# Decay projections from stacked rounded parts, head norms by logarithm and exponential, and a last feed-forward layer with tokens as rows

## The chip, the core and the metric

The kernel runs on one core of a Trainium2 chip and is one launch. The metric is device time in microseconds (us). The engines are TensorE (PE, its weight loads PEld), VectorE (DVE), ScalarE (ACT), GpSimd (POOL) and SyncE (SP), which here only issues transfers.

## The reference, cut to what matters

Two blocks of a language model run one after the other on x of 1024 tokens by 1024 features, all float32. Three places of them matter here.

```python
# block 1, gated linear attention, 4 heads: key width 128, value width 256
log_a_f = log_sigmoid(lr_f @ w_decay_up_fwd + b_decay_fwd) / 16    # lr_f: 1024 x 16
log_a_b = log_sigmoid(lr_b @ w_decay_up_bwd + b_decay_bwd) / 16    # rank 16 -> 512
o = o * rsqrt(mean(o * o, axis=-1) + EPS)                          # per head and token, 256 wide
o = o * gla_norm * silu(r)
# end of block 2
y = square(relu(m @ w_up)) @ w_down                                # 1024 -> 4096 -> 1024
x = x + rmsnorm_2(y, norm_post_mlp)                                # mean of squares over 1024 features
```

## The kernel before, in words

Activations lie with features on the 128 partitions and the 1024 tokens along the row. A float32 product is made of three products of rounded parts ("hi" and "lo", type fp32r): hi by hi, lo by hi, hi by lo. Small products are plain float32 matmuls. Each engine has its instructions in a written order; semaphores join them. SP issues nearly all transfers, and when it waits, all its later transfers wait too.

**Paired projections** (`in_pe`, `in_dve`, `in_act`, L1126, 49 to 262 us): the first projections go in pairs of column tiles by a scheme of seven products (numbers r = 0 to 6) instead of eight; DVE makes each product's weight remainder (`in_lo`, L1087) four products ahead. The first decay product (`decay`, L1311) of head 0 stands within the last pair.

**Gated heads** (`gla_pe`, `gla_act`, `gla_dve`, 262 to 608 us): per head, PE runs five other projections (`mid_unit`, L572) with the head's small products between them. Per head there are two `decay` products, each two float32 matmuls of 64 rows by 512 columns; the ACT chain Abs, Exp, Ln and a DVE scan follow. After `output`, ACT squares the two value halves, DVE adds them into `mn`, and within `mid_unit(h, 4)` PE sums them per token (`sum_tokens`, L608, at k = 3), DVE makes mean and reciprocal and lays them on a diagonal (L1713, L1716, L620), PE spreads that over the partitions (`spread_tokens`, L614, at k = 6), ACT takes the root (L1627), and DVE applies norm, gain and gate (L1729, L1733). Then the last unit is evacuated by DVE (`evacuate`, L680) and the next head begins.

**Second feed-forward** (`f2_*`, 2040 us to the end): 16 hidden pairs (P2 to P2O - 1), then 16 output pairs (P2O to P2_LAST), seven products of 128x512 each (L3972; twelve matmuls a product). POOL makes weight sums and, in the hidden pairs, the weights' lo parts (L3868); ACT the hi parts. In the hidden pairs DVE posts the results (L3988, L3995, L4004), applies relu and the token's scale (L4237), and makes four differences of hidden blocks (`mix2_dve`, L4107); SP stores seven hidden blocks a pair. The output pairs take w_down as the stationary side (with its sums) and the hidden blocks and their differences as the moving side ("operands", `operand_load`, `operand_hi`, `operand_lo` L4049), seven of them changed every four pairs.

**End**: the output has features on partitions. In the last pair PE turns it (`end_turn` L4415, `end_turn_block` L4471), sums squares over partitions (`end_sum` L4489), ACT evacuates, DVE scales and adds the residual by rows (`end_rows` L4514), and SP stores eight rows of 512 KB.

Of the kernel before, what the change touches and what calls it, by code (L numbers as in the profile page):

```python
# [18 lines left out]
ALU = mybir.AluOpType  # L19
# [22 lines left out]
            ("norm_post_mlp_2", 8), ("b_decay_fwd", 4), ("b_decay_bwd", 4), ("conv_w_2", 16),  # L42
# [91 lines left out]
OUT2 = ((0, 4), (1, 2), (5, 6), (3, 7))  # L134
# [90 lines left out]
class Step:  # L225
# [23 lines left out]
    def landed(self):  # L249
# [18 lines left out]
        " x_added out_t out_ev x3_turned x3_out lr_landed row_squared").split()  # L268
# [7 lines left out]
         "t_hi": ("osq_ready", 8), "t_lo": ("z_min", 8), "h_floor": ("o_norm", 16), "h_square": ("gates_sig", 16),  # L276
         "h_mixed": ("o_gate", 16), "op_hi": ("o_hi", 8), "op_lo": ("o_lo", 8), "y_gained": ("sc_ready", 8),
         "out_row": ("kdt_ready", 8), "x3_squared": ("g_step", 4), "x3_summed": ("conv_step", 16),
         "logs_summed": ("xt_tr", 8), "logs_exp": ("xt_ev", 8), "qw_exp": ("vec_t", 2),
         "conv_loaded": ("norm_row", 18),  # L280
         "qw_zero": ("consts_ready", 7), "qw_made": ("f_log", 3), "ones_set": ("yb_ready", 8),
         "kt_turned": ("yb_scaled", 8), "kw_made": ("o_sum", 8), "u_made": ("lat_sum", 4),
# [9 lines left out]
         "e_turned": ("rmask_ready", 2), "e_inverse": ("wup_zero", 1), "o_weighed": ("row_squared", 6),  # L292
         "e_stored": ("lr_landed", 18), "e_landed": ("pool_consts", 2),
         "x3_last_spilled": ("mv_loaded", 64)}
# [3 lines left out]
            ("gla_loaded", 64), ("wpool_loaded", 16))  # L298
# [9 lines left out]
def two_block_kernel(nc, A, out):  # L308
# [29 lines left out]
    hid_d = dram("hidden2", (CH2 * 7 * 4 * P, HALF))  # L338
# [5 lines left out]
    with ctx:  # L344
# [47 lines left out]
        esum = sb("exponential_sums", [P, 120])  # L392
# [12 lines left out]
        with ExitStack() as s:  # L405
# [11 lines left out]
            wup = sb("wup", [64, 2, HALF], F32, s)  # L417
# [47 lines left out]
        rstd2 = at("rstd2", [P, T], 0)  # L465
        sqa, sqb_, ssqA, ssqB = [at(n, [P, T], R0 + kb) for n, kb in
# [5 lines left out]
        sqe, ssqe = at("sq_end", [P, 2, T], R0), at("sq_sum_end", [P, T], R0 + 8)  # L472
        ytok = at("y_turned", [P, KT, C, P], R0 + 48)
        x3t = at("x_by_token", [P, C, T], R0 + 96)
        orow = at("out_rows", [P, 4, T], R0 + 80)
        mask_row = at("mask_row", [P, T], R0 + 128)
        ylast = at("y_last", [P, 2, HALF], R0 + 16)
# [133 lines left out]

        def spread_tokens(pe, pair, diagonal):
# [85 lines left out]
        N_CONST = 7  # L698

        def start_pool(pool):  # L700
# [10 lines left out]
                               pattern=[[1, P]], channel_multiplier=-1).then_inc(S["consts_ready"], 1)  # L711

# [312 lines left out]
        def in_sp(sp):  # L1025
# [3 lines left out]
            for p in range(N_INP):  # L1029
                if p + 2 < N_INP:  # L1030
                    in_pair_load(sp, p + 2)
# [58 lines left out]
        def in_pool(pool):  # L1090
# [3 lines left out]
            for p in range(N_INP):  # L1094
                for which in (1, 3, 2, 4):
                    in_sum(pool, p, which)
# [3570 lines left out]
```

## Time and profile before

| | us |
|---|---|
| median of 3 runs (range) | 2645.98 (2641.83 to 2646.13) |
| the profiled execution itself | 2648.13 |
| its span in the trace | 2646.4 |
| paired projections, about | 49 to 262 |
| gated heads | 262 to 608 |
| hidden pairs of the second feed-forward | 2040 to 2310 |
| output pairs and end | 2310 to 2646.4 |

The span is the trace's, from the first to the last instruction; the rest of the execution's 2648.13 lies around it. A busy PE counts overlapping matmuls: what one costs is read from the start of one row to the start of the next.

### The profile page before, as it was taken

How to read it: one execution, taken by the hardware profiler on the slowest of the kernel's cores; microseconds unless marked ns; L12 is line 12 of the kernel's file. 1: busy time of each engine (PE TensorE's matmuls, PEld its weight loads, DVE VectorE, ACT ScalarE, POOL GpSimd, SP SyncE). 2: the span in 40 equal slices, each digit the busy share in tenths (PEclk: the TensorE clock that was granted, in tenths of full speed). 3: DMA queues.
4: the chain of work that ended last, by engine and by line, in shares of the span. 5: the costliest groups of instructions: out<-in, count | busy, mean ns of one | idle time of the engine just before them, and what ended most of it. 6: DMA issues, size and time to landing. Idle time of an engine off the chain costs nothing.

```text
span 2646.4 us, 32521 instructions
## 1 busy us (share of the span) xinstructions
PE 2585.6 (98%) x12370; PEld 2089.4 (79%) x12370; DVE 1841.8 (70%) x2062; ACT 1032.6 (39%) x1435; POOL 1213.3 (46%) x761
## 2 busy tenths in 40 slices
PE   8999999999999999999999999999999999999998
PEld 6888788887787888887877888676886888877777
DVE  8666655547658666668879657666658666778787
ACT  6223344333124333334435111765455333434444
POOL 2222222233437888885333343241136888733331
PEclk9999999999999999999999999999999999999999
DMA  5333323245331433345642352402333555744443
GB/s 202 121 111 106 119 96 128 89 151 167 129 134 56 119 104 102 94 136 196 226 132 64 125 171 96 132 17 93 109 100 100 156 150 153 236 156 139 159 144 143
DMA packets 337168, 341.35 MB, mean 129 GB/s; under 512 B 20099, under 2 KB 255270, under 8 KB 337014
## 3 DMA queue, kind: packets, MB, share of 16 engines
q1 hardware_dynamic: 331798, 319.87, 38.4%
q10 hardware_dynamic: 5216, 19.40, 1.9%
q8 instruction: 100, 1.64, 0.3%
q14 instruction: 54, 0.44, 0.1%
HBM read 230.38 MB, written 107.80 MB: 128 GB/s over the span
## 4 chain that ended last, share of the span: by engine, by line
PE 54%; DVE 8%; issue 3%; DMA 2%; ACT 1%; POOL 1%; SPq 0%; DVEq 0%; ACTq 0%; POOLq 0%
PE ps L3972 37%; PE ps L572 9%; PE ps L2991 2%; DVE op_lo L4049 2%; PE ps L3035 1%; PE ps L3015 1%; DVE sw_lo L3868 1%; DMA op_raw<-hidden 1%; PE ps L3534 1%; PE ps L3919 1%; DMA x_block<-acc 1%; DVE acc L2443 0%; DVE acc L4302 0%; DVE acc L4295 0%; DMA w_raw<-in_w_uq 0%
## 5 line engine op out<-in xcount | busy, mean ns | idle before, releaser
L3972 PE MATMUL ps<-op_hi,sw_hi 128*128 128x512 f32 x1765 | 690.9, 391 | 17.0 <-DVE op_lo L4049 6.8
L3972 PE MATMUL ps<-op_hi,sw_lo 128*128 128x512 f32 x1765 | 687.6, 390 | 0.0
L3972 PE MATMUL ps<-op_lo,sw_hi 128*128 128x512 f32 x1765 | 687.5, 390 | 0.0
L3972 PEld LDWEIGHTS ps<-op_hi,sw_hi 128*128 128x128 f32 x1765 | 331.7, 188 | 98.1 <-issue 16.6
L3972 PEld LDWEIGHTS ps<-op_hi,sw_lo 128*128 128x128 f32 x1765 | 331.7, 188 | 69.1
L3972 PEld LDWEIGHTS ps<-op_lo,sw_hi 128*128 128x128 f32 x1765 | 331.8, 188 | 68.6 <-issue 0.5
L538 POOL TENSOR_TENSOR w_hi_t<-w_raw,ones 128x1024 fp32r<-128x1024 f32 (+1 forms) x58 | 107.3, 1854 | 508.6 <-DMA w_raw<-in_w_in 242.2
L3858 ACT ACTIVATE sw_hi<-sw_sumNone 128x512 fp32r<-128x512 f32 (+1 forms) x252 | 157.0, 624 | 331.9 <-PE ps L3972 237.4
L3868 POOL TENSOR_TENSOR sw_lo<-sw_sumNone,sw_hi 128x512 fp32r<-128x512 f32 x138 | 214.4, 1563 | 34.5 <-ACT sw_hi L3858 34.4
L3819 POOL TENSOR_TENSOR sw_sumNone<-sw_raw 128x512 f32<-128x512 f32 (+1 forms) x63 | 113.9, 1808 | 227.4 <-DVE sw_lo L3868 196.8
L3858 ACT ACTIVATE sw_hi<-sw_raw 128x512 fp32r<-128x512 f32 (+1 forms) x188 | 116.8, 622 | 196.3 <-PE ps L3972 194.7
L3868 POOL TENSOR_TENSOR sw_lo<-sw_raw,sw_hi 128x512 fp32r<-128x512 f32 x109 | 157.8, 1449 | 53.2 <-ACT sw_hi L3858 53.2
L542 POOL TENSOR_TENSOR w_lo_t<-w_raw,w_hi_t 128x1024 fp32r<-128x1024 f32 (+1 forms) x58 | 151.0, 2607 | 4.1
L3834 POOL TENSOR_TENSOR sw_sumNone<-sw_raw,sw_sumNone 128x512 f32<-128x512 f32 (+1 forms) x63 | 92.0, 1461 | 87.5 <-DVE sw_lo L3868 84.8
L4004 DVE TENSOR_TENSOR hidden_blocks<-ps,s_u 128x512 f32<-128x512 f32 x111 | 76.1, 686 | 77.1 <-PE ps L3972 76.7
L3826 POOL TENSOR_TENSOR sw_sumNone<-sw_sumNone,sw_raw 128x512 f32<-128x512 f32 (+1 forms) x63 | 100.7, 1598 | 62.8 <-DVE sw_lo L3868 60.0
L4049 DVE TENSOR_TENSOR op_lo<-op_raw,op_hi 128x2048 fp32r<-128x2048 f32 (+1 forms) x49 | 119.6, 2443 | 6.8 <-ACT op_hi L4042 6.8
L3988 DVE TENSOR_TENSOR s_u<-ps,s_p 128x512 f32<-128x512 f32 x65 | 44.8, 689 | 110.1 <-PE ps L3972 110.0
L572 PE MATMUL ps<-m2hi,w_hi_t 128*128 128x512 f32 x304 | 106.4, 406 | 4.6 <-DVE m2lo L1546 2.1
L680 DVE TENSOR_TENSOR stage<-ps,rstd 128x1024 f32<-128x1024 f32 x36 | 43.9, 1220 | 90.2 <-PE ps L572 85.1
L572 PE MATMUL ps<-h1hi,w_hi_t 128*128 128x512 f32 x320 | 103.2, 404 | 0.0
L572 PE MATMUL ps<-m2lo,w_hi_t 128*128 128x512 f32 x304 | 101.7, 390 | 0.0
(514 smaller groups left out, 5415.5 us busy)
## 6 DMA issues: line engine op xcount, KB each, us to landing
op_raw<-hidden SPq DMA_DIRECT2D x42, 1024.0 KB, 8.9
w_raw<-in_w_in SPq DMA_DIRECT2D x47, 512.0 KB, 4.7
sw_raw<-in_w_ffn_in SPq DMA_DIRECT2D x44, 512.0 KB, 5.2
hidden<-hidden_blocks SPq DMA_DIRECT2D x13, 1536.0 KB, 6.1
hidden<-hidden_blocks SPq DMA_DIRECT2D x14, 1280.0 KB, 5.0
sw_raw<-in_w_up SPq DMA_DIRECT2D x32, 512.0 KB, 8.5
sw_raw<-in_w_down SPq DMA_DIRECT2D x32, 512.0 KB, 5.3
acc<-proj SPq DMA_DIRECT2D x28, 512.0 KB, 4.5
```

Of the source, the lines that this page charges most:

```text
L538: ins = pool.tensor_tensor(whi[:, u.par, s], raw[:, u.par, s], ones[:, 0:1].to_broadcast([P, n]), ALU.mult)
L542: ins = pool.tensor_tensor(wlo[:, u.par, s], raw[:, u.par, s], whi[:, u.par, s].bitcast(F32), ALU.subtract)
L572: mm = pe.matmul(out[:, b * HALF:(b + 1) * HALF], w, x[:, k, b * HALF:(b + 1) * HALF], start=(begin and k == ks[0] and n == 0), stop=(end ...
L2991: mm = pe.matmul(PS[n % 2][:, b:b + w], qT[0:96, h, i * P:(i + 1) * P], kT[0:96, h, b:b + w], start=True, stop=True)
L3819: pool.tensor_tensor(s1, a21, a22, ALU.add).then_inc(S["sw_sum"], 1)
L3826: pool.tensor_tensor(s2, s1, a11, ALU.subtract).then_inc(S["sw_sum"], 1)
L3834: pool.tensor_tensor(s2, a12, s2, ALU.subtract).then_inc(S["sw_sum"], 1)
L3858: act.activation(wshi[ring(m)][:, 0:n], weight_block(p, r), ACT.Copy).then_inc(S["sw_hi"], 1)
L3868: eng.tensor_tensor(wslo[ring(m)][:, 0:n], weight_block(p, r), wshi[ring(m)][:, 0:n].bitcast(F32), ALU.subtract).then_inc(S["sw_lo"], 1)
L3972: mm = pe.matmul(out, w, x[:, k, :], start=(k == 0 and i == 0 and r < 4), stop=(k == n - 1 and i == 2), skip_group_check=r >= 4)
L4004: dve.tensor_tensor(out, bank(p, r), u[:, :], ALU.add).then_inc(S["s_post"], 1)
L4049: dve.tensor_tensor(lo_of(first, r)[:, :, :], fresh_of(first, r)[:, :, :], hi_of(first, r)[:, :, :].bitcast(F32), ALU.subtract).then_inc(S ...
```

## The change

The decay columns: the low-rank activations are rounded once into `lr_parts` (128 rows: rounded part twice for the two weight parts already stacked, then its remainder, then the rounded part again), the decay weights into `w_parts` of the same 128 rows, by four ACT and three DVE instructions within the paired projections; `decay` becomes two fp32r matmuls of 128 rows by 512 columns. POOL clears `wup` once more and SP issues four more weight loads before pair 6's. In `in_dve` two evacuations and a small product change places around `t_lo(3)`.

The head norm: PE multiplies the squares by a matrix of ones on the stationary side (`spread_sums`, two float32 matmuls of 512 columns, at k = 3), which sums and spreads at once; ACT takes Ln with the mean's scale and the epsilon as bias, then Exp with scale -0.5. `sum_tokens`, `spread_norm`, and DVE's three instructions go.

The last layer: the hidden tiles are stored once (no differences) and loaded as the stationary side; w_down is the moving side, three of its blocks directly, four as differences that DVE makes in the hidden pairs (`down_load`, `down_mix`, `down_store`, one buffer). The output has tokens on partitions. So the squares' sums come from ACT's accumulator, root and reciprocal are of one column, the gain is a row loaded once, and the rows are finished and stored tile by tile in the last pairs. All turns and sums at the end go. Besides, four loads of block 2's value tiles are issued earlier (`mlstm_sp`), one vector is no longer turned, and semaphore counts move; these are left out below.

```diff
-OUT2 = ((0, 4), (1, 2), (5, 6), (3, 7))
+OUT2 = ((0, 4), (1, 5), (2, 6), (3, 7))
...
+        def spread_sums(pe, pair, squares):
+            for b in range(2):
+                mm = pe.matmul(PS[pair][:, b * HALF:(b + 1) * HALF], ones[:, :],
+                               squares[:, b * HALF:(b + 1) * HALF], start=True, stop=True)
+            return mm
...
-                    pe.wait_ge(S["gla_loaded"], 64)
-                    pe.wait_ge(S["unit_out"][0], 1)
+                    pe.wait_ge(*count("lr_part", 7))
...
+                if r == 4 and p in (1, 2, 6):
+                    (lr_high, lr_rounded, None, None, None, wup_rounded)[p - 1](act)
...
-                mm = pe.matmul(decay_bank(h, d)[:, b * HALF:(b + 1) * HALF], wup[:, d, h * P:(h + 1) * P],
-                               lrT[:, b * HALF:(b + 1) * HALF], start=True, stop=True)
+                mm = pe.matmul(decay_bank(h, d)[:, b * HALF:(b + 1) * HALF], w_parts[:, d * HALF + h * P:d * HALF + (h + 1) * P],
+                               lr_parts[:, b * HALF:(b + 1) * HALF], start=True, stop=True)
...
+        def lr_high(act):
+            act.wait_ge(S["unit_out"][0], 1)
+            act.activation(w_parts[0:64, :], lrT, ACT.Copy).then_inc(S["lr_part"], 1)
...
+        def lr_low(dve):
+            dve.wait_ge(*count("lr_part", 1))
+            dve.tensor_tensor(lr_parts[64:96, :], lrT[0:32, :], w_parts[0:32, :].bitcast(F32), ALU.subtract)\
...
+        def lr_rounded(act):
+            act.wait_ge(*count("lr_part", 2))
+            act.activation(lr_parts[0:64, :], lrT, ACT.Copy).then_inc(S["lr_part"], 1)
+            act.wait_ge(S["gla_loaded"], 64)
+            act.wait_ge(*count("lr_part", 3))
+            act.activation(lr_parts[96:P, :], w_rows[96:P, :], ACT.Copy).then_inc(S["lr_part"], 1)
...
+            dve.wait_ge(*count("lr_part", 4))
+            dve.tensor_tensor(w_parts[96:P, :], w_rows[96:P, :], lr_parts[96:P, :].bitcast(F32), ALU.subtract)\
+               .then_inc(S["lr_part"], 1)
+            dve.wait_ge(*count("lr_part", 5))
+            dve.tensor_copy(lr_parts[96:P, :], lr_parts[0:32, :].bitcast(F32)).then_inc(S["lr_part"], 1)
...
+            act.activation(w_parts[0:96, :], w_rows[0:96, :], ACT.Copy).then_inc(S["lr_part"], 1)
...
-                sum_tokens(pe, 3, [mn]).then_inc(S["o_sum"], 1)
-            def spread_norm(h):
-                pe.wait_ge(S["o_norm"], 4 * h + 4)
-                spread_tokens(pe, 3, mn).then_inc(S["o_sum"], 1)
+                spread_sums(pe, 3, mn).then_inc(S["o_sum"], 1)
-                mid_unit(h, 4, lambda k: square_sum(h) if k == 3 else spread_norm(h) if k == 6 else None)
+                mid_unit(h, 4, lambda k: square_sum(h) if k == 3 else None)
...
-                act.wait_ge(S["o_sum"], 2 * h + 2)
-                act.activation(mn[:, :], PS[3][:, :], ACT.Sqrt).then_inc(S["o_rstd"], 1)
+                if h == 0:
+                    act.wait_ge(S["consts_ready"], N_CONST + 1)
+                act.wait_ge(S["o_sum"], h + 1)
+                act.activation(mn[:, :], PS[3][:, :], ACT.Ln, scale=1.0 / 256, bias=eps).then_inc(S["o_norm"], 1)
+                act.wait_ge(S["o_norm"], 2 * h + 2)
+                act.activation(mn[:, :], mn[:, :], ACT.Exp, scale=-0.5).then_inc(S["o_rstd"], 1)
-                dve.wait_ge(S["o_sum"], 2 * h + 1)
-                dve.tensor_scalar(tok(0), by_tile(PS[3][:, :])[:, :, 0:1], 1.0 / 256, EPS, ALU.mult, ALU.add)\
-                   .then_inc(S["o_norm"], 1)
-                dve.wait_ge(S["o_norm"], 4 * h + 2)
-                dve.reciprocal(tok(0), tok(0)).then_inc(S["o_norm"], 1)
-                dve.wait_ge(S["o_norm"], 4 * h + 3)
-                diagonal(dve, mn[:, :], 0).then_inc(S["o_norm"], 1)
...
-                    out.append((w_down, (n1 * P, n2 * P), 8 * c, 4))
+                    out.append((hid2, (n1 * P, n2 * P), 8 * c, 4))
...
+            elif r in DOWN_BLOCK:
+                i, half = DOWN_BLOCK[r]
+                src = w_down[:, 8 * c + 4 * i:8 * c + 4 * i + 4, half]
+            else:
+                row = (4 * c + DOWN_DIFF.index(r)) * 4 * P
+                src = down_d[row:row + 4 * P, :].rearrange("(k p) t -> p k t", p=P)
...
-                    sp.wait_ge(*count2("h_mixed", 4 * (q + 1)))
-                    hidden_store(sp, q, q // 4, q % 4)
+                if 0 <= q < P2O - P2:
+                    sp.wait_ge(*count2("h_square", 4 * (q + 1)))
+                    sp.dma_start(hid2_tiles[q // 4, q % 4], hb2[q % 2][:, :, :]).then_inc(S["hid_stored"][q % 2], 16)
+                    if q < N_DOWN - 2:
+                        down_load(sp, q)
...
+                if p == P2O:
+                    down_load(sp, N_DOWN - 2)
+                if 0 <= q < N_DOWN - 2:
+                    down_store(sp, q)
+                if p == P2O + 1:
+                    down_store(sp, N_DOWN - 2)
+                    down_load(sp, N_DOWN - 1)
+                if p == P2O + 2:
+                    down_store(sp, N_DOWN - 1)
+                if p >= N_PAIR - 4:
+                    end_rows_sp(sp, p - N_PAIR + 4)
...
+        def down_load(sp, q):
+            if q:
+                sp.wait_ge(S["down_stored"], 32 * q)
+            for i in range(2):
+                sp.dma_start(wdown[i][:, :], down_tiles[q // 4, q % 4][:, i, :]).then_inc(S["down_landed"], 16)
...
+        def down_store(sp, q):
+            c, k = q // 4, q % 4
+            sp.wait_ge(*count("down_mixed", 4 * (q + 1)))
+            dst = down_d[16 * c * P:16 * (c + 1) * P, :].rearrange("(r k p) t -> p r k t", r=4, k=4)[:, :, k, :]
+            for i in range(2):
+                sp.dma_start(dst[:, 2 * i:2 * i + 2, :], wdown[i][:, :].rearrange("p (r t) -> p r t", r=2))\
+                  .then_inc(S["down_stored"], 16)
...
+        def down_mix(dve, q, steps):
+            blocks = {r: wdown[i // 2][:, HT[i % 2]] for i, r in enumerate(DOWN_DIFF)}
+            if steps[0] == 0:
+                dve.wait_ge(S["down_landed"], 32 * (q + 1))
+            for i in steps:
+                o, y = ((3, 2), (1, 3), (2, 1), (5, 1))[i]
+                if i in (1, 2, 3):
+                    dve.wait_ge(*count("down_mixed", 4 * q + min(i, 2)))
+                dve.tensor_tensor(blocks[o], blocks[o], blocks[y], ALU.subtract).then_inc(S["down_mixed"], 1)
...
-                if m in (N_SEQ - 6, N_SEQ - 5, N_SEQ - 3):
-                    n = 2 * (N_SEQ - 6, N_SEQ - 5, N_SEQ - 3).index(m)
-                    end_turn(pe, n)
-                    end_turn(pe, n + 1)
-                if m == N_SEQ - 2:
-                    end_turn_block(pe, 0)
-                    end_turn_block(pe, 1)
-                    end_sum(pe, 0)
-                    end_turn_block(pe, 2)
...
+            t = p - 1 - (N_PAIR - 4)
+            if t == 2:
+                for e in (4, 5):
+                    end_gain(dve, e)
+                for e in (4, 5):
+                    end_inverse(dve, e)
+                end_row(dve, 4)
...
-                end_adds(dve, p - 1)
+            if p in (P2O + 1, P2O + 2):
+                down_mix(dve, N_DOWN - 2 + p - P2O - 1, (0, 1, 2, 3))
+            if 0 <= t < 2:
+                end_gain(dve, 2 * t)
+            if p == P2_LAST:
+                end_block_gain(dve, 0)
...
-                end_gain(dve, 2)
-                end_scale(dve, 0)
-                end_rows(dve, 0, 2)
+                end_block_gain(dve, 2)
+                end_inverse(dve, 6)
+                end_row(dve, 6)
...
+                act.activation(sqe[:, :], acc[:, END_TILES[e], :], ACT.Square, accum_out=square_of(e)).then_inc(S["sq_done"], 1)
...
+            act.activation(deviation(e), square_of(e), ACT.Sqrt, scale=1.0 / D, bias=bias_of(e)).then_inc(S["rstd_ready"], 1)
...
+            dve.tensor_tensor(y_row(e), y_row(e), gain_row[:, :], ALU.mult).then_inc(S["y_gained"], 1)
...
+            dve.scalar_tensor_tensor(out=y_row(e)[:, a], in0=y_row(e)[:, a], scalar=inverse_of(e), in1=x3_row(e)[:, a],
+                                     op0=ALU.mult, op1=ALU.add).then_inc(S["out_row"], 1)
```

## Rows read from the trace of the kernel before

**Rows 1.** The page's parts 1 and 4: busy shares; the chain that ended last.
```profile
PE 2585.6 (98%) x12370; PEld 2089.4 (79%) x12370; DVE 1841.8 (70%) x2062; ACT 1032.6 (39%) x1435; POOL 1213.3 (46%) x761
...
PE 54%; DVE 8%; issue 3%; DMA 2%; ACT 1%; POOL 1%; SPq 0%; DVEq 0%; ACTq 0%; POOLq 0%
```

**Rows 2.** Windows view: span, then busy PE, PEld, DVE, ACT, POOL, clock, DMA.
```profile
62.00:249.00 187.00, 187.00 (x826) 154.89 (x826) 114.81 (x162) 47.85 (x78) 48.61 (x38) 1.00 0.39 121
...
276.00:362.00 86.00, 84.91 (x443) 70.54 (x444) 47.86 (x50) 33.38 (x31) 18.94 (x9) 1.00 0.32 104
...
2040.00:2310.00 270.00, 270.00 (x1191) 223.38 (x1192) 186.90 (x192) 107.54 (x175) 228.13 (x153) 1.00 0.57 174
```

**Rows 3.** Timeline of PE, first head: start, length, line, tile, count.
```profile
318.24 1.98 PE L1311 MATMUL ps<-ssq,wup 64*128 64x512 f32 x4
320.15 0.73 PE L572 MATMUL ps<-h1hi,w_hi_t 128*128 128x512 f32 x2
...
339.65 1.95 PE L608 MATMUL ps<-ones,mn 128*128 128x128 f32 x16
341.35 0.71 PE L572 MATMUL ps<-h1hi,w_hi_t 128*128 128x512 f32 x2
341.89 0.62 PE L572 MATMUL ps<-h1lo,w_hi_t 128*128 128x512 f32 x2
342.35 0.61 PE L572 MATMUL ps<-h1hi,w_lo_t 128*128 128x512 f32 x2
```

**Rows 4.** Timelines of ACT and DVE around the first head's norm.
```profile
322.49 1.28 ACT L1566 ACT_TABLE_LOAD   x1
...
347.44 1.03 ACT L1627 ACTIVATE mn<-ps 128x1024 f32<-128x1024 f32 x1 [6.14 <-PE ps L614]
...
348.50 1.28 DVE L1729 SCALAR_TENSOR_TENSOR kd<-ps,cols,mn 128x1024 f32<-128x1024 f32 x1 [5.21 <-ACT mn L1627]
```

**Rows 5.** Timeline of PE: waits at two head boundaries (in brackets).
```profile
364.72 1.09 PE L1459 MATMUL ps<-ident,kd 128*128 128x128 f32 x8 [1.00 <-DVE kd L1674]
...
609.31 0.73 PE L572 MATMUL ps<-m2hi,w_hi_t 128*128 128x512 f32 x2 [1.32 <-DVE stage L680]
```

**Rows 6.** Timelines of DVE and PE where the paired projections begin.
```profile
58.26 2.47 DVE L997 TENSOR_TENSOR acc<-ps,rstd 128x512 f32<-128x512 f32 x4
...
61.50 0.47 PE L1126 MATMUL ps<-h1hi,w_hi_t 128*128 128x512 f32 x1 [1.26 <-issue]
```

**Rows 7.** DMA issues, 2040 to 2310 us: KB each, median us to landing; DVE's mixes by form.
```profile
sw_raw<-in_w_up SPq DMA_DIRECT2D x26, 512.0 KB, 8.8
...
hidden<-hidden_blocks SPq DMA_DIRECT2D x7, 1280.0 KB, 5.0
...
L4107 DVE TENSOR_TENSOR hidden_blocks<-hidden_blocks,hidden_blocks 128x512 f32<-128x512 f32 x14 | 22.3, 1591 | 0.5
```

**Rows 8.** The end: two pieces of the chain, then timelines of PE and DVE, then DMA.
```profile
2610.49 1.75 PE ps L4415 x16
2612.23 2.74 PE ps L3972 x12
...
2626.54 0.60 PE L4471 MATMUL ps<-ident,acc 128*128 128x128 f32 x4
...
2629.95 0.48 PE L3972 MATMUL ps<-op_hi,sw_hi 128*128 128x512 f32 x1
...
2632.56 0.39 PE L3972 MATMUL ps<-op_hi,sw_lo 128*128 128x512 f32 x1
...
2638.09 4.87 DVE L4514 SCALAR_TENSOR_TENSOR out_rows<-y_turned,bytok,x_by_token 128x1024 f32<-128x1024 f32 x4 [0.81 <-ACT y_turned L4478]
...
out<-out_rows SPq DMA_DIRECT2D x8, 512.0 KB, 2.7
```

More of the change, by code:

```diff
@@ L698, in two_block_kernel @@
         N_CONST = 7
+        eps = small[:, 56:57]
         def start_pool(pool):
@@ L4218, in f2_act @@
                         square_act(act, p, i - 3)
-                    if p == P2_LAST:
-                        if i in (3, 4):
-                            end_block_act(act, i - 3)
-                        if i in (1, 2, 4):
-                            for n in range(2):
-                                end_evict(act, 2 * (1, 2, 4).index(i) + n)
+                    if p == P2_LAST and i in (3, 4):
+                        end_block_square(act, i - 3)
                 if p < P2O:
                     square_act(act, p, 3)
-        def mix2_dve(dve, q, steps):
-            dve.wait_ge(*count2("h_square", 4 * q + 4))
-            mix(dve, q, BEFORE2["h_mixed"] + 4 * q, steps)
         def hidden_dve(dve, p):
@@ L4481, in end_sum @@
-        def end_sum(pe, h):
-            pe.wait_ge(S["sq_added"], POST + 8)
-            pe.wait_ge(*count("s_post", posted(P2_LAST, "11")))
-            for n, src in enumerate((ssqe[:, HT[h]], block_square(2 + h))):
-                if n:
-                    pe.wait_ge(S["sq_done"], POST + 9 + h)
-                for c in range(4):
-                    mm = pe.matmul(PS[2][:, (4 * h + c) * P:(4 * h + c + 1) * P], src[:, c * P:(c + 1) * P], ones[:, :],
-                                   start=(n == 0 and c == 0), stop=(n == 1), skip_group_check=True)
-            mm.then_inc(S["norm_sum"], 1)
@@ new lines, in end_rows_sp @@
+        def end_rows_sp(sp, t):
+            if t == 0:
+                sp.wait_ge(*count("s_product", done(N_PAIR - 5, 6)))
+                sp.dma_start(gain_row[:, :], A["norm_post_mlp_2"][0].rearrange("(o n) -> o n", o=1).to_broadcast([P, T]))\
+                  .then_inc(S["gain_landed"], 16)
+                for e in range(2):
+                    x3_load(sp, e)
+                return
+            if t == 3:
+                sp.wait_ge(*count("s_product", done(P2_LAST, 0)))
+                for e in (6, 7):
+                    x3_load(sp, e)
+            for e in (2 * t - 2, 2 * t - 1):
+                row_store(sp, e, e)
+                if t < 3:
+                    x3_load(sp, e + 2)
@@ L4539, in end_sp @@
+            end_inverse(dve, 7)
+            for h in range(2):
+                end_row(dve, 7, h)
         def end_sp(sp):
-            for c in range(C):
-                sp.wait_ge(*count("out_row", c + 1))
-                sp.dma_start(out[0, c * P:(c + 1) * P, :], orow[:, c % 4, :]).then_inc(S["out_stored"][c % 4], 16)
+            row_store(sp, 6, 6)
+            for h in range(2):
+                row_store(sp, 7 + h, 7, HT[h])
             for i in range(4):
-                sp.wait_ge(S["out_stored"][i], 16 + 16 * C // 4)
+                sp.wait_ge(S["out_stored"][i], 16 + 16 * ((9 + 3 - i) // 4))
```

356 lines of the change are left out of this document (175 added, 181 removed).

## The prediction

> **What bounds the kernel now.** I read the page's busy shares first: PE is busy 98% of the span, DVE 70%, POOL 46% [rows 1]. The chain that ends last runs on PE for 54% of the span, and none of its other engines has more than 8% [rows 1]. The view by windows shows where another engine could take over: in the paired projections PE is busy 187.0 of 187 us with DVE at 115 and ACT at 48, around the first gated head 84.9 of 86 with DVE at 47.9, and of the second feed-forward 270.0 of 270, with POOL at 228 and DVE at 187 [rows 2]. So a matmul that leaves PE is worth its whole slot, provided that what follows it on ACT and DVE does not become late, and anything that delays PE in the hidden pairs is a loss. Only the last 13.5 us, behind the last product (2632.56 + 0.39 = 2632.95), are not PE's: there DVE writes rows and the stores land [rows 8].
>
> **Decay columns.** One decay product takes PE from 318.24 to 320.15, 1.91 us [rows 3]. It becomes two fp32r matmuls of 512 columns, the same as a pair of L572 matmuls, whose starts lie 342.35 - 341.89 = 0.46 us apart [rows 3]. Saved: 1.45 us, eight times = 11.6 us. Bounds for the new product, which the trace does not have: 0.46 us, and 1.91 us if it were no faster than the float32 one; I take the near row, since form and columns are those of L572. The new preparation is four ACT and three DVE instructions of up to 1024 columns. An ACT pass of that width is 1.03 us, a DVE one 1.28 [rows 4]. They stand at five places in a stretch where ACT is busy 48 and DVE 115 of 187 us [rows 2], and a remainder is made some three products of 2.7 us ahead of its use; that lead hides them, and I cost them at nothing. Without that cover they would cost 4 x 1.03 + 3 x 1.28 = 8 us. SP's four extra issues come while it waits for the sixth pair's slot anyway. POOL's second clearing stands between two pairs' sums.
>
> **Start of the paired projections.** PE waits 1.26 us until 61.50 for DVE's next remainder, which comes behind four evacuation halves (58.26 + 2.47 = 60.73) [rows 6]. Two of the halves now stand before `t_lo(3)`, in an idle spot, two behind the remainder. Bounds 0 and 1.26; I take 1.2.
>
> **Head norm on PE.** The sum per token costs 341.35 - 339.65 = 1.70 us and lengthens the next pair to 0.54 (341.89 - 341.35) instead of 0.46: 1.78 [rows 3]. The new matmuls have the form of the old spread, two float32 ones of 512 columns against ones, only earlier and with the sides changed. So one of the two steps goes, and the other stays at its price. Saved 1.78 us, four times = 7.1; bounds 0 (if the new step cost both) and 1.91, the other float32 pair of that width [rows 3].
>
> **Head norm on ACT and DVE.** Before, the root starts at 347.44 and ends at 348.47, and DVE, after 5.21 us of waiting, applies the norm at 348.50 [rows 4]. Now the sums are ready at 341.4; Ln of about 1.05 ends at 342.6; a table load of 1.28 [rows 4] and Exp of about 1.05 follow: 345.0. So DVE is 3.5 us earlier against PE, where PE itself comes 1.8 us earlier. The table load between the two is what the trace shows between Exp and Ln in the decay chain (322.49) [rows 4]. The Trainium skill, "ScalarE: Activation LUTs", section "Table sets: the hidden batching unit", says that one set holds both ln and exp, one load for the two. By that rule the norm would be ready 1.28 us sooner still, and the sum would be the same, since PE does not wait for it. The existing Exp and Ln show a load between them, so I follow the row.
>
> **What is late next in the heads.** At a head's start PE waits 1.00 us for `kd`, behind the evacuation of the unit that PE has just finished [rows 5]. That moves with PE and stays. After the last head PE waits 1.32 us for an evacuation [rows 5], which also follows its own unit; there ACT must do five more passes, two loads, Ln and Exp, and ends about when the evacuation does. I cost that at 0, bounds 0 and 1.3. Heads and projections together: 11.6 + 7.1 + 1.2 = 19.9 us.
>
> **The last layer, product by product.** Numbers and shapes of products, weight sums and operands are unchanged, so are DVE's four differences a pair, and the stationary side is still 512 KB a tile. In the hidden pairs SP now stores 1 MB of hidden tiles and moves 1 MB of w_down in and out, where before it stored 1.8 MB: 1.2 MB more a pair of 19 us, at a DMA share of 0.57 [rows 2]. One buffer serves load, mix and store, so there is a loop. With 5.0 us for a store of 1.3 MB [rows 7] a store takes about 4.5 us and a load of 1 MB about as long. From the first mix, which is behind the fifth product, to the last, 6.7 us go by (four at 1.59 [rows 7] and small gaps). Sum 15.7, below the pair's 19.0 (7 products of 2.72). Upper bound: 7 for the store, 8.8 for the load (the weights' landing) [rows 7], 7.3 for the mixes at 1.59 each: 23. I take no loss. The differences for the last two tiles go behind products in the second and third output pair; the two-pair margin hides them. The value tiles' earlier loads of block 2 wait for nothing PE needs: 0.
>
> **The end.** In the last pair PE turns three times two tiles at 1.75 us each and then spends 2629.95 - 2626.54 = 3.4 us on the block turns and sums [rows 8]: 8.7 us that go. The pair's products take 7 x 2.72 (a product is 2.74 in the chain [rows 8]) = 19.0 us, so it starts at T0 = 2632.95 - 19.0 - 8.7 = 2605. DVE comes into it at about T0 + 3.3, behind the fourth row. Its new order before the last post: two gains of 1.22 (4.87 / 4, [rows 8]), four small steps of 0.2, three rows of 1.28, and fourteen half-width steps (remainders, posts, half gains) of 0.65 (2.47 / 4 = 0.62 for such a one, [rows 6]): 2.4 + 0.8 + 3.8 + 9.1 = 16.1. That is T0 + 19.4; with some 1 us of waits within I take T0 + 20.4, 1.4 us behind the last product. Then post 0.7, ACT's last half square about 0.8 with its readout, root 0.2, reciprocal 0.2, two half rows 1.4: T0 + 23.7. From the last row to the end went 2646.4 - (2638.09 + 4.87) = 3.4 us; a store lands in 2.7 [rows 8], and a half one in no more: 3.2. End at T0 + 26.9 = 2631.9: 14.5 us saved. Bounds: 16 if DVE is on time and the half store quicker, 8.7 - 1.5 = 7 if the new tail is as long as the old one and DVE delays PE in it.
>
> **Sum.** 19.9 + 14.5 = 34.4 us off the profiled execution's 2648.1 gives 2613.7; the median of the runs is 2.1 below that execution, so 2612 us (2645.98 - 34.4 = 2611.6).
>
> **Rivals.**
> - A, the loop of load, mix and store is longer than a pair. For it: a single buffer, and 8.8 us landings [rows 7]; against it: most bytes are in rows of 2 and 4 KB, and the weights' loads come after the new load. Each us above 19.0 costs 14 us over the hidden pairs, less some 6.5 us of DVE's lead (about 2.4 products of 2.72, an estimate). At 20.5 us a pair: 14.5 lost, 2626. From 19.0 + (34.4 + 6.5) / 14 = 21.9 us on, the kernel is slower than before; at the upper bound of 23 it loses 49.5 us: 2661. That is the case of the other sign.
> - B, the heads keep less of what PE gives up: the chain from decay to `ks`, or the weights' load and split behind the evacuations, becomes the bound at each head. For it: PE already waits at each head's start [rows 5]; against: those waits follow PE's own units. If half of the heads' 18.7 goes, 2621.
> - C, the new end is DVE's: gains and rows (8 passes more over three pairs) delay posts, and PE waits. 5 to 7 us of the 14.5 lost: 2618.
> - D, the stacked product is no faster (it does not do what it says): 11.6 lost, 2623.
> - E, two input passes of DVE collide less or more with POOL than now: a mix has 1.59 us against 0.62 for a half-width step elsewhere [rows 6, 7]. This is within +-3 of the forecast.
>
> **How the numbers follow.** Forecast with E: 0.68, own range 2607 to 2617. B 0.09, C 0.10, D 0.03, A mild (2615 to 2640) 0.06, A slow 0.04. The range reaches from 2606 to 2624, which leaves out the slow cases and the strong forms of B and D. About 0.2% can be told from no change (5 us). Faster: 0.95; within: 0.01; slower: 0.04.
>
> **What would show it.** Decay rows of PE with next starts 0.46 us on; no L608 in the heads; Ln and Exp of 1.05 us with a table load between them and DVE's norm 3.5 us closer to the sum; waits at `kd` as now; PE busy 270 of 270 in the hidden pairs with no wait on a posted block, and down loads that land before DVE's fifth post; from the last product to the end 7 to 8 us instead of 13.5. The prediction is wrong if PE shows waits in the hidden pairs, or if the last pair takes more than 20 us.

## The result, and the profile after

The changed kernel takes 2615.44 us (median of 4 runs, 2612.77 to 2617.83) where the kernel before takes 2646.0. The ratio is 0.9889, 95% interval 0.9874 to 0.9905. The forecast was 2612, its range 2606 to 2624. The profiled execution took 2615.75 us with a span of 2614.0, 32.4 less than before in both, where 34.4 was forecast.

The busy shares hardly move: PE stays at 98% and lost 34 us of busy time; DVE gained 16. Columns are those of [rows 1].

```profile
PE 2551.7 (98%) x12194; PEld 2066.4 (79%) x12194; DVE 1857.9 (71%) x2060; ACT 1026.0 (39%) x1442; POOL 1214.3 (46%) x763
```

The windows that answer to [rows 2]: the paired projections, the first head, the hidden pairs, and the start of the output pairs.

```profile
62.00:249.00 187.00, 186.78 (x825) 154.62 (x825) 120.98 (x165) 53.07 (x84) 50.67 (x39) 1.00 0.39 119
276.00:362.00 86.00, 83.94 (x446) 71.33 (x445) 48.56 (x47) 37.28 (x35) 26.21 (x12) 1.00 0.37 119
2020.00:2290.00 270.00, 269.64 (x1190) 223.28 (x1191) 196.44 (x187) 102.18 (x171) 226.85 (x152) 1.00 0.67 226
2290.00:2340.00 50.00, 43.74 (x169) 32.26 (x168) 36.18 (x39) 18.19 (x23) 12.20 (x8) 0.97 0.68 231
```

Within these 270 us the hidden pairs are as full of PE as before, with the DMA share at 0.67 instead of 0.57. The fourth row is new: of 50 us PE is idle 6.3, and the granted clock is 0.97 of full. That is where the change loses.

The same matmul, found in both traces, shows where the 32.4 us come from. A product starts with the first of its matmuls.

| PE reaches | before | after | gained so far |
|---|---|---|---|
| second product of the paired projections | 61.50 | 59.17 | 2.3 |
| end of the last head | 605.53 | 587.79 | 17.7 |
| first hidden pair | 2036.46 | 2013.48 | 23.0 |
| first output pair's operands | 2314.83 | 2293.25 | 21.6 |
| its first products over | 2331.22 | 2314.70 | 16.5 |
| the end of the last product | 2632.95 | 2606.79 | 26.2 |
| end of the span | 2646.4 | 2614.0 | 32.4 |

The third place lies at a wait that only the kernel before has there. The changed kernel has one of its own two products later. The first row is the kernel before, the second the changed one:

```profile
2036.46 0.50 PE L3972 MATMUL ps<-op_hi,sw_hi 128*128 128x512 f32 x1 [1.49 <-DVE s_u L3995]
```
```profile
2020.36 0.47 PE L4040 MATMUL ps<-op_hi,sw_hi 128*128 128x512 f32 x1 [1.28 <-issue]
```

Ahead of the first row the gain is 21.3, at its start 23.0, and behind the second row it is 22.3, where it stays to the end of the hidden pairs. The profile names no releaser for the second wait; POOL's `sw_lo` had ended 0.1 us before it did (2020.26).

The timeline of PE, first head, in answer to [rows 3]. The decay product and the head norm's only product:

```profile
313.84 0.62 PE L1339 MATMUL ps<-lr_parts,wup_parts 128*128 128x512 f32 x2
314.29 0.62 PE L580 MATMUL ps<-h1hi,w_hi_t 128*128 128x512 f32 x2
...
333.65 1.88 PE L623 MATMUL ps<-mn,ones 128*128 128x512 f32 x4
334.96 1.03 PE L580 MATMUL ps<-h1hi,w_hi_t 128*128 128x512 f32 x2
```

The next pair follows the decay product after 314.29 - 313.84 = 0.45 us instead of 1.91. The new norm product shows as four pieces and holds PE 1.3 us until the next pair's first start, and that pair is lengthened to 0.87.

ACT and DVE around the norm, in answer to [rows 4]:

```profile
335.61 1.28 ACT L1694 ACT_TABLE_LOAD   x1 [1.60 <-PE ps L623]
336.90 1.11 ACT L1694 ACTIVATE mn<-ps,small 128x1024 f32<-128x1024 f32 x1
338.04 1.28 ACT L1696 ACT_TABLE_LOAD   x1
339.33 1.06 ACT L1696 ACTIVATE mn<-mn 128x1024 f32<-128x1024 f32 x1
...
340.43 1.28 DVE L1791 SCALAR_TENSOR_TENSOR kd<-ps,cols,mn 128x1024 f32<-128x1024 f32 x1 [7.34 <-ACT mn L1696]
```

There is a table load before Exp, as forecast, and one more before Ln, which the forecast left out: in this head it stands behind ACT's wait for PE. The load before Exp is one that the rule weighed in the prediction (the Trainium skill, "ScalarE: Activation LUTs", section "Table sets: the hidden batching unit") would not have; by the row it is there, 1.28 us. Against PE's next pair DVE applies the norm 340.43 - 334.96 = 5.5 us later, where before it was 348.50 - 341.35 = 7.2 [rows 3, 4]: 1.7 closer, not 3.5.

The waits of PE, summed (us in total, times, longest), and two waits at the start of the second head, in answer to [rows 5]:

```profile
PE ps L4040 <- DVE op_lo L4127: 9.1, 9, 3.7
PE ps L1528 <- DVE kd L1743: 4.5, 4, 1.8
...
PE ps L1536 <- ACT vtok L1637: 2.3, 3, 0.8
```
```profile
356.63 1.09 PE L1528 MATMUL ps<-ident,kd 128*128 128x128 f32 x8 [0.70 <-DVE kd L1743]
359.85 3.26 PE L1536 MATMUL ps<-vtok,kdtok 128*128 128x256 f32 x14 [0.78 <-ACT vtok L1637]
```

The second wait did not exist before, and in all there are three of it. Between the turned values and the products that use them PE had a decay product of 1.9 us; ACT needs 1.02 us for the evacuation in between, and a product of 0.45 no longer covers it.

DVE at the end, in answer to [rows 8]:

```profile
2606.62 0.17 DVE L4570 RECIPROCAL bytok<-bytok 128x1 f32<-128x1 f32 x1 [0.39 <-ACT bytok L4530]
2606.87 1.28 DVE L4577 SCALAR_TENSOR_TENSOR y_last<-y_last,bytok,x_by_token 128x1024 f32<-128x1024 f32 x1
2608.07 0.68 DVE L4403 TENSOR_TENSOR acc<-ps,acc 128x512 f32<-128x512 f32 x1
...
2610.13 1.41 DVE L4577 SCALAR_TENSOR_TENSOR y_last<-y_last,bytok,x_by_token 128x512 f32<-128x512 f32 x2
```

PE's last product ends at 2606.79, its post starts 1.3 us later behind a row of another tile, and the end is 2614.0 - 2606.79 = 7.2 us behind the product, where before it was 13.5.

### The profile page after: what moved, and what is told of

Same layout as the page of the kernel before. It is cut to its first block and busy times, and to the rows that moved or that the text cites. A ratio compares the mean times of both kernels' runs of the same rounds, so it can differ in the third digit from the quotient of the medians.

```text
span 2614.0 us, 32217 instructions
## 1 busy us (share of the span) xinstructions
PE 2551.7 (98%) x12194; PEld 2066.4 (79%) x12194; DVE 1857.9 (71%) x2060; ACT 1026.0 (39%) x1442; POOL 1214.3 (46%) x763
## 3 DMA queue, kind: packets, MB, share of 16 engines
q8 instruction: 98, 1.61, 0.3%
## 5 line engine op out<-in xcount | busy, mean ns | idle before, releaser
L4040 PE MATMUL ps<-op_hi,sw_hi 128*128 128x512 f32 x1765 | 690.8, 391 | 18.9 <-DVE op_lo L4127 9.1
L3936 POOL TENSOR_TENSOR sw_lo<-sw_sumNone,sw_hi 128x512 fp32r<-128x512 f32 x138 | 219.7, 1601 | 20.9 <-ACT sw_hi L3926 20.3
L3887 POOL TENSOR_TENSOR sw_sumNone<-sw_raw 128x512 f32<-128x512 f32 (+1 forms) x63 | 107.7, 1709 | 224.0 <-DVE sw_lo L3936 188.8
L580 PE MATMUL ps<-m2hi,w_lo_t 128*128 128x512 f32 x304 | 101.5, 389 | 0.0
```

The costliest lines, as they stand in the source:

```text
L580: mm = pe.matmul(out[:, b * HALF:(b + 1) * HALF], w, x[:, k, b * HALF:(b + 1) * HALF], start=(begin and k == ks[0] and n == 0), stop=(end ...
L3887: pool.tensor_tensor(s1, a21, a22, ALU.add).then_inc(S["sw_sum"], 1)
L3936: eng.tensor_tensor(wslo[ring(m)][:, 0:n], weight_block(p, r), wshi[ring(m)][:, 0:n].bitcast(F32), ALU.subtract).then_inc(S["sw_lo"], 1)
L4040: mm = pe.matmul(out, w, x[:, k, :], start=(k == 0 and i == 0 and r < 4), stop=(k == n - 1 and i == 2), skip_group_check=r >= 4)
```

## The experiments

Each series ran with the kernel before beside it (medians 2644.6 to 2646.1 us). The changed kernel itself ran beside the first series only, so the others are set against both of its medians, 2615.44 and 2617.6. Places on PE's timeline are from one execution of each kernel. "Net of the clock" means that the stretches at half clock, told of with the first run, are taken out at half their length: within one, matmuls of 512 columns start 0.43 us apart instead of 0.23.

**The changed kernel again.** No edit.

> The changed kernel once more, as the measure for the others of this series. Both theories: 2612 to 2618 us, ratio 0.9885 to 0.9895 to the kernel before. It tells what is lasting in the 5.7 us that PE gains between 605 and 2036 us of the kernel before, where the forecast had none. Theory 'chance': most are stretches at half clock that fall by accident (the kernel before had 3.4 us of it at 847 and 6.8 us at 1813, the changed one none and 3.4), so this execution has other ones and the gain there moves by 1 to 3 us. Rival 'early value tiles': the earlier loads of the value tiles make it, so it is again 5 to 6 us.

Measured: 2617.6 us (2616.7 to 2618.9), ratio 0.9892. Its profile loses 3.1 us against the first one by two steps on PE, both at stretches where the granted clock is half: one at 440.9 and one at 830.1. Such stretches last 3.4, 6.8 or 10.2 us. The kernel before has these (the clock is the third number from the end):

```profile
847.03:850.44 3.41, 3.41 (x10) 2.67 (x9) 3.31 (x4) 0.08 (x1) 3.33 (x3) 0.50 0.00 0
1696.95:1700.36 3.41, 3.41 (x9) 1.91 (x8) 1.20 (x5) 2.22 (x8) 0.00 (x0) 0.50 0.87 323
1813.00:1819.83 6.83, 6.62 (x29) 4.89 (x31) 4.29 (x12) 3.35 (x6) 2.36 (x2) 0.50 0.01 2
```

The changed kernel has three of 3.41 us (1676.6, 1792.7, 2311.5), and this second execution of it five. Net of them the two executions agree within 0.4 us at every place of the table above (17.8 and 17.9 gained at the end of the heads, 19.6 and 19.7 at the first hidden pair). So of the 5.2 us between the heads and the hidden pairs 3.4 are the clock, as the theory 'chance' had it; that they fell by accident is likely from these two executions, not shown. Of the other 1.8, which both executions have, 1.5 are the wait of the kernel before at this very place, and most of it is paid back by the wait two products later. The rival 'early value tiles' falls with the run of the heads alone below.

**Decay products in float32.**

```diff
-pe.matmul(decay_bank(h, d)[...], w_parts[:, d * HALF + h * P:...], lr_parts[:, ...])
+pe.matmul(decay_bank(h, d)[...], w_parts[0:64, d * HALF + h * P:...].bitcast(F32), lr_parts[0:64, ...].bitcast(F32))
```

> The changed kernel with the decay products as float32 matmuls of 64 rows again; all preparation of the stacked rows stays, the remainders are left out of the product. Theory 'slot less cover': eight products 1.45 to 1.55 us longer (11.6 to 12.4), less the three waits of 0.78 us for the value tile that the longer product covered: 9.5 us slower than the changed kernel, about 2625. Rival 'whole slot': 12 us slower, 2627.5. Rival 'no faster': no difference, 2615.5.

Measured: 2623.56 us, 6.0 above the run of the changed kernel beside it (8.1 above its first median); ratio 0.9916 (0.9903 to 0.9930). At the end of the heads PE is 8.8 us behind the changed kernel, net of the clock, near the 9.5 of the theory. The steps are 1.55 to 1.61 us at each plain product, and PE no longer waits for the value tile; `kd`'s waits shrink too:

```profile
PE ps L1528 <- DVE kd L1743: 3.2, 4, 1.8
```

The median moved less because this kernel's execution has only one stretch at half clock (6.8 us) where the changed one beside it has 17.1. "No faster" falls, and "whole slot" is 3 us too high for the trace, 6 for the median.

**The head norm as before.** The edit takes back `spread_sums`, Ln and Exp, and brings back `sum_tokens`, `spread_norm`, Sqrt and DVE's three instructions.

> The changed kernel with the head norm as before: sums at k = 3, DVE's mean, reciprocal and diagonal, spread at k = 6, root on ACT. Theory 'PE slots': four sums of 1.48 to 1.78 us come back: 6 to 7 us slower than the changed kernel, about 2622. Rival 'earlier norm': the norm's earlier end is worth something of its own (the next head's first waits shrink), then 8 us or more slower. Rival 'hidden': under 3 us.

Measured: 2627.95 us, 10.3 above the run of the changed kernel beside it (12.5 above its first median); ratio 0.9931 (0.9918 to 0.9943). At the end of the heads the cost is 6.1 us net of the clock: the four sums, less 1.4 of `kd` waits that this kernel does not have. That is the forecast's term. Of the rest 1.7 are half clock and some 2.2 lie in the last pair and behind it, where nothing of the edit is. There DVE stood waiting for a row of the residual, whose load landed 6.5 us after its issue, where in the changed kernel it took 3.9:

```profile
2607.32 1.28 DVE L4584 SCALAR_TENSOR_TENSOR acc<-acc,bytok,x_by_token 128x1024 f32<-128x1024 f32 x1 [2.27 <-DMA x_by_token<-x_after_mixer]
```

Why this load is slower here stays open. The rival "earlier norm" has the median for it but not the trace: in the heads nothing beyond the slots is lost.

**Only the heads.** The kernel before with the two head parts, the last layer as it was.

> The kernel before with only the two head parts of the change: stacked decay products and the norm by ones, logarithm and exponential; the last layer and the value tiles' loads as before. Theory 'parts add': the heads' 15 us and the start's 2.3: 17.3 less than before, about 2629, ratio 0.9935. Rival 'forecast as written': 19.9 less, 2626. Rival 'they interact' (the end was the whole gain, or the earlier heads are eaten later by waits of block 2): under 12 us less, over 2634.

Measured: 2627.9 us, 18.2 below the kernel before; ratio 0.9930 (0.9918 to 0.9943). PE has gained 17.5 at the end of the heads and, net of the clock, 18.0 at the first hidden pair. So the heads' part gives alone what it gives in the whole change and makes 18 of its 28.5 us in this series. Just ahead of that place the changed kernel stands at 17.9 too, net of the clock. So the earlier loads of the value tiles, which this kernel does not have, are worth nothing there. The 1.6 us that the whole change shows more at the first hidden pair (19.6 against 18.0) are the wait told of above, and two products later 0.9 are left (18.9 against 18.0). The rest of the series' 28.5, some 10 us, is the last layer's part, which was forecast at 14.5; no run has that part alone.

**Each store of differences twice.**

```diff
+for i in (0, 1):
+    sp.dma_start(again[:, 2 * i:2 * i + 2, :], wdown[i][...]).then_inc(S["down_stored"], 16)
 for i in (0, 1):
     sp.dma_start(dst[:, 2 * i:2 * i + 2, :], wdown[i][...]).then_inc(S["down_stored"], 16)
```

> The changed kernel with every store of w_down's differences issued twice (the first copy to a place that nothing reads). In the changed kernel's trace the loop of one buffer is: store 4.2 us, load 6.1, four mixes with the posts between them 7.7: 18.0 us of the pair's 19.0. Theory 'loop nearly full': a second store adds 3 to 4 us, the loop becomes 21 to 22 us, each of some 13 pairs grows by 2 to 3 us less what DVE has in hand: 20 to 35 us slower than the changed kernel, 2636 to 2652, with PE waiting on posted blocks in the hidden pairs. Rival 'loop as forecast, 15.7 us': the second store fits, at most 3 us slower, under 2621. Rival 'DMA share': the 1 MB more slows the weights' landings instead, waits on landings rather than on posts.

Measured: 2626.01 us, 8 to 11 above the changed kernel's two medians; ratio 0.9931 (0.9916 to 0.9946). Both the theory's 20 to 35 and the rival's 3 are wrong in size. Of the 10.7 us between the two profiled executions 5.1 are half clock (20.5 us of it against 10.2), and some 5 are lost in the hidden pairs, nearly all in their last six. DVE now waits for 13 of the 14 loads, 48.2 us in all, as the theory had it.

```profile
2234.93 1.35 DVE L4266 TENSOR_TENSOR down_low_rows<-down_low_rows 128x512 f32<-128x512 f32 x1 [6.05 <-DMA down_high_rows<-in_w_down]
...
2254.03 1.27 DVE L4266 TENSOR_TENSOR down_low_rows<-down_low_rows 128x512 f32<-128x512 f32 x1 [4.76 <-DMA down_high_rows<-in_w_down]
...
2258.62 0.68 DVE L4266 TENSOR_TENSOR down_low_rows<-down_low_rows,down_high_rows 128x512 f32<-128x512 f32 x1
2259.22 0.68 DVE L4266 TENSOR_TENSOR down_high_rows<-down_high_rows 128x512 f32<-128x512 f32 x1
```

SP's issues and their landings in this trace: the stores take 7.0 us (2240.53 to 2247.50), the load 6.5, and from the first mix to the last only 5.9 instead of 7.7, for the last two mixes take 0.68 us each where in the changed kernel they take 1.77. So the loop is 19.4 us, hardly above the pair's 19.0. A DVE that waits works at other moments and its passes get shorter; that gave back 1.8 of the 3 us that the stores added. Of the last six pairs three or four lose some 0.4 us each, as the loop is longer than the pair; one loses 1.3 and the last 2.4.

What PE waits for is not a posted block, as the theory said. At each of the places where it falls behind, it starts at most 0.11 us after POOL has ended a lo part of the weights (`sw_lo`). Two rows ahead of one such place and the sum of POOL's waits (29.8 us in the changed kernel) show one way there:

```profile
2239.33 0.63 ACT L4304 ACTIVATE hidden_rows<-hidden_rows 128x512 f32<-128x512 f32 x1 [6.75 <-DVE hidden_rows L4343]
...
2240.56 1.29 POOL L3936 TENSOR_TENSOR sw_lo<-sw_sumNone,sw_hi 128x512 fp32r<-128x512 f32 x1 [3.14 <-ACT sw_hi L3926]
```
```profile
POOL sw_lo L3936 <- ACT sw_hi L3926: 52.5, 25, 3.1
```

A late DVE holds ACT at the hidden rows, ACT's next `sw_hi` comes late, and with it POOL's `sw_lo`. The third rival is not ruled out beside it: the weights land in 7.5 us (median) instead of 6.1.

**Root and reciprocal in place of logarithm and exponential.**

```diff
-act.activation(mn, PS[3], ACT.Ln, scale=1.0 / 256, bias=eps)
-act.activation(mn, mn, ACT.Exp, scale=-0.5)
+act.activation(mn, PS[3], ACT.Sqrt, scale=1.0 / 256, bias=eps)
+dve.reciprocal(mn, mn)
```

> The changed kernel with the sums and spreads by ones as it has them, but Sqrt on ACT (same scale and epsilon) and a reciprocal of 128x1024 on DVE in place of Ln and Exp. Theory 'the matmul is the gain': PE's slots are the same, and it stays within 2 us of the changed kernel, 2615.5 to 2619. Rival 'logarithm and exponential matter': DVE has a pass more before the norm, the next head's first scan and evacuation come later, 3 us or more slower.

Measured: 2625.41 us, 8 to 10 above the changed kernel's two medians; ratio 0.9928 (0.9910 to 0.9945). The theory is wrong and the rival holds: PE's slots are the same, but DVE's reciprocal of 1024 columns is long.

```profile
340.03 6.55 DVE L1785 RECIPROCAL mn<-mn 128x1024 f32<-128x1024 f32 x1 [4.93 <-ACT mn L1694]
```

At the start of the next head PE waits for this reciprocal, 4.2 us in three heads, and behind the last head 7.0 us for `m2lo`, which DVE makes after it; its waits for `kd` fall from 4.5 to 1.0. Net of the clock the traces differ by 3.4 us at the last product (5.4 if the part of a stretch in which PE is idle anyway is not counted). The rest is half clock, 27.3 us of it against 10.2, and two of its stretches begin 0.6 us behind the wait of 2.28 at 346.6 and within the one of 7.0. So summing and spreading in one product needs an inverse that is wide, and Ln and Exp make it for 1.1 us each, and two table loads of 1.28, on an engine that has time. The old order paid 0.20 us for a reciprocal of 8 columns.

**The output pairs' operands first.** In the changed kernel SP issues the loads of the first output pair's operands here (start, length of the issues):

```profile
2274.81 0.48 SPq L4249 DMA_DIRECT2D down_differences<-down_high_rows  x1
2275.33 3.01 SPq L4115 DMA_DIRECT2D op_raw<-down_differences  x3
2278.38 0.90 SPq L4220 DMA_DIRECT2D hidden<-hidden_rows  x1
2281.30 7.03 SPq L3864 DMA_DIRECT2D sw_raw<-hidden  x2
2288.38 3.36 SPq L4115 DMA_DIRECT2D op_raw<-in_w_down  x1
```

The first row is the second half of a store that waits for DVE's last mix. The loads stand behind it, then go out in one bunch, and the weights' issue takes 7 us. The waits that follow on PE:

```profile
2297.38 0.47 PE L4040 MATMUL ps<-op_hi,sw_hi 128*128 128x512 f32 x1 [1.16 <-DVE op_lo L4127]
...
2312.01 0.77 PE L4040 MATMUL ps<-op_hi,sw_hi 128*128 128x512 f32 x1 [3.74 <-DVE op_lo L4127]
```
```diff
-if 0 <= q < N_DOWN - 2:
+if 0 <= q < N_DOWN - 3:
     down_store(sp, q)
+if p == P2O - 1:
+    down_store(sp, N_DOWN - 3)
```

> The changed kernel with one store of differences (the third from last tile's) moved on SP behind the first output pair's operand loads and weights, where in the changed kernel it stands ahead of them and holds them until DVE's mix at 2274.4. Theory 'SP order': the loads go out some 2.4 us earlier and not in one bunch, the operand waits of 3.7 and 1.2 us around 2297 to 2312 shrink to the 1.3 of the kernel before and the half clock behind them goes: 3 to 5.5 us faster than the changed kernel, 2611 to 2614. Rival 'bandwidth': the loads of 1 MB land late because of the bytes, whatever their order: under 1 us.

Measured: 2611.16 us (2610.5 to 2612.0), ratio 0.9873 (0.9858 to 0.9887), 4.3 below the changed kernel's first median and 6.4 below its second. The loads start at 2272.54 and the weights' issue takes 1.9 us:

```profile
2272.54 5.80 SPq L4115 DMA_DIRECT2D op_raw<-down_differences  x3
...
2282.96 1.91 SPq L3864 DMA_DIRECT2D sw_raw<-hidden  x2
```

PE's waits for operands fall from 9.1 to 5.3 us, the longest from 3.7 to 1.1, the half clock at 2311 is gone, and PE is 4.3 us ahead behind the place, net of the clock. The theory holds.

**`kd` before the evacuation.** DVE in the changed kernel, then in this one:

```profile
353.31 1.23 DVE L695 TENSOR_TENSOR stage<-ps,rstd 128x1024 f32<-128x1024 f32 x1 [1.99 <-PE ps L580]
354.45 2.13 DVE L1743 TENSOR_TENSOR kd<-acc,mn 128x1024 f32<-128x1024 f32 x1
```
```profile
351.64 1.23 DVE L1741 TENSOR_TENSOR kd<-acc,mn 128x1024 f32<-128x1024 f32 x1
353.63 1.23 DVE L695 TENSOR_TENSOR stage<-ps,rstd 128x1024 f32<-128x1024 f32 x1 [0.77 <-PE ps L580]
```
```diff
-if d == 0:
-    evacuate(h, 0)
 dve.wait_ge(S["e_ready"], m + 4)
 ...
 dve.tensor_tensor(kd, gk, Ering[1], ALU.mult)
 if d == 0:
+    evacuate(h, 0)
     gate_min(dve, h, 1)
```

> The changed kernel with DVE making kd before it evacuates the head's first unit, where PE waits for kd 0.7 to 1.8 us at each of four head starts (4.5 us in all). Theory 'the evacuation is what kd waits for': 2.5 to 4.5 us faster, 2612 to 2615. Rival 'next in line': the evacuation, 2 us later, makes PE or the weights' split wait instead, no gain within 1 us, or slower.

Measured: 2609.53 us (2608.5 to 2614.6), ratio 0.9871 (0.9854 to 0.9888), 5.9 below the changed kernel's first median and 8.1 below its second. The waits for `kd` are gone from PE and 4.4 us more are gained at the end of the heads; the waits for the value tile stay (2.5 us). The pass is also shorter, 1.23 us for 2.13. The theory holds.

**Rounded sums.**

```diff
-dve.tensor_tensor(mn, qs, ks, ALU.add)
+dve.tensor_tensor(mn_r, qs, ks, ALU.add)        # mn_r: the same place, fp32r
-pe.matmul(PS[pair][...], ones, squares[...])
+pe.matmul(PS[pair][...], ones_r, squares[...])  # ones_r: ones in fp32r
```

> The changed kernel with the squares rounded as they are added and the ones as a rounded tile, so that the head norm's two matmuls of 512 columns are fp32r ones. Theory 'a slot less its cover': each goes from some 1.9 us to 0.46, four times = 5.8, less what the waits at the next head's start take: 4 to 6 us faster than the changed kernel, 2610 to 2613.5. Rival 'kd bounds the heads': kd's waits (4.5 us) grow by as much as PE gains: under 1.5 us.

Measured: 2612.08 us, ratio 0.9871 (0.9858 to 0.9885), 3.4 below the changed kernel's first median and 5.5 below its second. PE gains 7.5 us by the end of the heads (25.3 for 17.7), more than the theory had: the product now takes 0.45 us, and the waits for `kd` fall from 4.5 to 1.4, where the rival had them grow. Then four stretches at half clock of 20.5 us in all, 10.2 of them in one at 1671.7, give back 5.1 more than the changed kernel's. The rival falls. The median alone shows half of what the edit gives in the heads.

**The two orders together, and all three edits.**

> The changed kernel with both orders mended, kd before the first unit's evacuation and the store of differences behind the output pairs' operand loads; the arithmetic is the changed kernel's. Theory 'both add': 4.2 us (heads) and 4.4 us (operands), with some 1.7 for a stretch at half clock that goes: 8.5 to 10.5 us faster than the changed kernel, 2605 to 2609. Rival 'only the larger': 2609 to 2611.

> Both orders mended and the rounded sums. Theory 'all add': 13 to 16 us faster than the changed kernel, 2600 to 2604, ratio to the kernel before 0.983 to 0.985. Rival: the rounded sums' part is eaten by the waits for the value tile and kd, then as the two orders alone, 2605 to 2609.

Measured: the two orders 2605.63 us (2603.5 to 2607.7), ratio 0.9846 (0.9832 to 0.9859); all three edits 2601.45 us (2601.2 to 2602.5), ratio 0.9832 (0.9818 to 0.9845). Both theories hold. The last one is 44.6 us below the kernel before and 14 to 16 below the changed one.

## Why the prediction was right, step by step

- **Decay columns, 11.6 us.** The slot was right: 0.45 us for each product, steps of 1.55 to 1.61, for the long product also lengthened the pair behind it. What was missed is what the long product covered: three waits of 0.8 us for the value tile, one of 0.6 for `kdtok`, and part of `kd`'s. In the float32 run the first two are gone and `kd`'s are 1.3 us shorter, and by the heads of that one trace the part is worth 8.8, not 11.6 (6.0 and 8.1 by the medians). Rival D, no faster, is out. The three DVE and four ACT preparations cost nothing that PE shows (186.8 of 187 us busy).
- **Start, 1.2 us.** PE gained 1.4 there, and 0.9 earlier by an input's landing, which varies from run to run (0.1 to 0.9).
- **Head norm, 7.1 us.** The run with the old norm gives 6.1, for the four sums of 1.78 are less 1.4 of waits for `kd`. DVE came 1.7 us closer to PE in the first head, not 3.5, above all for Ln's own table load of 1.28, which stands behind the wait. PE did not wait for that.
- **"What is late next", 0 us.** This is the step that failed, by some 3 us: the prediction said that `kd`'s wait moves with PE and stays. PE gained 15.4 of the 18.7 between the start and the end of the heads. Rival B is of this kind, at a third of its price, but it named the chain to `ks` and the weights' split; what became late is the value tile on ACT and `kd` on DVE.
- **The hidden pairs, 0 us.** Right in the sum, and by the sign that the prediction itself named, waits of PE in the hidden pairs, not wholly: PE is busy 269.6 of 270 us, but its wait of 1.28 us that ends at 2020.36 lies mostly ahead of that window. Against it stand the waits of 1.5 and 0.3 us that the kernel before has there, so the entry gained 1.0. The loop was put at 15.7 us and is 18.0 (store 4.2, load 6.1, mixes with the posts between 7.7), so the margin to the pair's 19.0 was 1 us and not 3.3. At a loop of 19.4 the price was some 5 us of work in the run with doubled stores. The term that was mis-sized is the stretch from the first mix to the last, 7.7 for 6.7. The mixes themselves take 1.6 us in the mean, as forecast (1.2, 1.7, 1.8 and 1.8 in one pair); DVE's other steps between the second and the third were put at "small gaps" and take 1.6. Rival A did not come, and had less far to come than the prediction thought.
- **The start of the output pairs, not in the sum.** This is the largest error, 5.8 us: 4.2 of waits and 1.6 of clock, from 22.3 us gained at the end of the hidden pairs to 16.5. The run with the operands first gives 4.3 of it back. The prediction looked at the issues that the change adds within a pair, and not at what SP has queued behind the last store of the hidden pairs.
- **The end, 14.5 us.** PE enters the last pair 17.3 us ahead. The pair gave 26.2 - 17.3 = 8.9 where 8.7 was forecast, the tail 6.2 where 5.8 was: the post came 1.3 us behind the product (1.4 forecast), the end 7.2 us (8). Rival C is out.
- **The middle, 0 us.** Between the heads and the hidden pairs 3.6 us came that were not in the forecast, 3.4 of them by the clock. With the two losses they make the sum nearly right: -3.3 (heads), +1.1 (start), +3.6, +1.0 (entry of the hidden pairs), -5.8, and +1.4 behind them are the 2.0 us between 34.4 and 32.4. That the number is better than its steps is luck.

## What to carry to other kernels

When a matmul gets shorter, read what runs under it on the other engines: here a product of 1.9 us hid an evacuation of 1.02, and a fifth of what was saved came back as waits. A wait can also cost twice: of what the wide reciprocal and the doubled stores cost in their profiled executions, about half or more was half clock, part of it right behind the new waits. When a queue gets a transfer that waits for late data, list what stands behind it at the phase's last turn, not in the middle of the phase. And before a difference of two medians is given to an edit, take the stretches at half clock out of both traces.

## What the hardware showed that was not expected

- The granted clock falls to half (1.2 GHz of 2.4) for 3.4, 6.8 or 10.2 us, at one to seven places of an execution before its last product. Two that were looked at stand at a wait: 2.6 us of it ahead of the one at 847, 3.74 us ahead of and into the one from 2311.5 to 2314.9. But a wait of 2.8 us that ended at 828.2 in the changed kernel had none behind it, and in its other execution the same wait, 2.7 us, had one. The kernels shown lose between 3.4 and 13.7 us by them, as much as one part of the change is worth.
- A reciprocal on DVE of 128x1024 takes 6.55 us, five times a multiplication of that size (1.28).
- The same DVE pass over 512 columns, the third and fourth mix, takes 0.68 or 1.77 us. In the changed kernel's hidden pairs POOL is at work during each of the long ones; in the run with doubled stores twelve pairs have short ones, and POOL stands idle during every one of them.
- An issue of SP's takes 0.4 us with few transfers outstanding and up to 6.6 us when some 4.5 MB are (2281.71 to 2288.34 in the changed kernel).
